# Block 1's first feed-forward products by Strassen's algorithm: pairs of output tiles in seven products of quarters

## The chip, the core and the metric
The kernel runs on one core of a Trainium2 chip. Its time is the device time of one launch in microseconds (us), the median of several runs. In the texts PE is TensorE, which multiplies matrices; ACT is ScalarE, DVE is VectorE, POOL is GpSimd, and SP is SyncE, which issues the loads of the weights. Every engine works through a list of instructions of its own, and the engines wait for each other by counting semaphores.

## What is computed
Two transformer blocks follow each other on one sequence of 512 tokens with 1024 features. The change touches the feed-forward layer of the first block, where `w_ff1` is 1024 by 4096 and `w_ff2` is 4096 by 1024:

```python
x = x + merged @ w_out[l]
h = rms_norm(x, g_mlp[l])
x = x + jnp.square(jax.nn.relu(h @ w_ff1[l])) @ w_ff2[l]
```

## The kernel before
**Halves.** Everything is float32. For a product of two matrices each operand is split in a high part that TensorE's fp32r format holds, and the rest. A product then takes three matmuls: high times high, weights' high times input's low, weights' low times input's high. The split of a weight tile costs one cast on ACT (raw `WR` to `WH`, L1226) and one subtraction on DVE (`WL = WR - WH`, L1691). There are four raw buffers `WR0` to `WR3` and three places for halves. A tile of weights is 128 by 1024 numbers.

**Order.** `tile_list` gives the order of all weight tiles: the output projection `wo` 0 to 7, then four quarters, each of 8 tiles `f1` and 8 tiles `f2`, then block 2. SP loads a tile as soon as the tile four before it has been split. ACT and DVE run two tiles ahead of PE with `split_to(tid[...] + 2)`, called at fixed places of their lists.

**Block 1's feed-forward.** A tile `f1, n` gives 128 hidden features for all 512 tokens: 8 chunks of 128 input features, three matmuls of 512 columns each, in PSUM bank 2 + n % 4. The input's halves are `Ah` and `Al`, made from x with its gain by `raw_high` (ACT, L1233) and `raw_low` (DVE, L1700) as the tiles of `wo` are added to x (DVE, L2037). The norm's factor is applied later, in the ReLU (DVE, L2172). It comes late: PE sums the squares in the middle of `f1` 0 and 1 (`sums("m1")`, the matmuls on ONE), DVE takes the variance (L1707), ACT a logarithm and an exponential (`root`, L1256 and L1258), DVE three operations of a Newton step (L1720 to L1724). ACT squares twice (L1528, and L1532 into `Bh`), DVE subtracts (`Bl`, L2177). The tiles `f2` multiply `Bh` and `Bl`, and DVE adds them to x (L2191).

**POOL** adds the squares of `wo`'s tiles for the norm (`add_squares`, L2381) and has nothing to do from there to the end of the third quarter.

## Time and profile before

| | |
|---|---|
| median of 3 runs | 1615.81 us (1610.54, 1617.73, 1615.81) |
| the profiled execution's own time | 1613.71 us |
| its span, first to last instruction | 1611.9 us |
| mean granted TensorE clock | 0.977 of 2.4 GHz |
| PE busy | 1542.1 us, 96% |
| DVE busy | 823.0 us, 51% |
| ACT busy | 617.6 us, 38% |
| POOL busy | 393.2 us, 24% |
| DMA | 154.11 MB, mean 96 GB/s |

Busy time is the share of the span in which an engine had an instruction in work. Matmuls overlap, so the time between the starts of two of them says more than the length of one. The chain of waits follows the end of the program back from each instruction to what released it.

### The profile page before, as it was taken

The page shows a single profiled execution, that of the slowest core. Times are in us where ns is not written, and L with a number is a line of the kernel's source. Part 1 is how long each engine was busy: PE and PEld are TensorE (multiplying, and loading weights), DVE is VectorE, ACT ScalarE, POOL GpSimd, SP SyncE. Part 2 cuts the span into 40 slices and gives each one's busy share as a digit, 9 for nine tenths or more (in the row PEclk, how much of TensorE's full clock was granted, in tenths as well). Part 3 has the DMA queues.
Part 4 walks back from the last instruction along what each step waited for, and adds up shares of the span by engine and source line. Part 5 has one row for each costly group of instructions (what it writes and reads, how often), then busy time and mean ns, then how long its engine had stood idle before and what let it go on. Part 6 is the DMA issues. An engine that isn't in the chain of part 4 may idle for free.

```text
span 1611.9 us, 19519 instructions
## 1 busy us (share of the span) xinstructions
PE 1542.1 (96%) x7198; PEld 1225.1 (76%) x7202; DVE 823.0 (51%) x1644; ACT 617.6 (38%) x1118; POOL 393.2 (24%) x364
## 2 busy tenths in 40 slices
PE   6899989999999999999999999989999999999995
PEld 5687665688877888888888788756687888888884
DVE  5537566444444334343446697577363543443444
ACT  5424456522334223232355433555443321322222
POOL 3200554300020000000036634566541210220112
PEclk9899999999999999999999999989999999999998
DMA  5743300323322333332322653311422333232321
GB/s 190 129 112 92 105 1 14 104 92 103 93 83 87 96 95 97 93 103 92 102 89 79 154 148 118 111 40 60 157 80 90 92 97 99 92 104 92 100 82 54
DMA packets 46669, 154.11 MB, mean 96 GB/s; under 512 B 5698, under 2 KB 5890, under 8 KB 46576
## 3 DMA queue, kind: packets, MB, share of 16 engines
q1 hardware_dynamic: 41840, 137.63, 27.2%
q0 software_dynamic: 4736, 15.25, 4.4%
q8 instruction: 58, 0.95, 0.3%
q14 instruction: 35, 0.29, 0.1%
HBM read 142.78 MB, written 9.55 MB: 95 GB/s over the span
## 4 chain that ended last, share of the span: by engine, by line
PE 86%; DVE 7%; ACT 3%; issue 2%; DMA 1%; DVEq 0%; SPq 0%; another core or an unknown queue 0%; POOL 0%; ACTq 0%
PE PSA L578 84%; PE PSA L780 2%; DVE WL L1691 1%; ACT AR L1298 1%; DVE AHL L1897 1%; DMA WR<-w_in 1%; PE PSA L924 0%; ACT AHL L1346 0%; DVE AR L1781 0%; DVE AR L1779 0%; DVE AR L1806 0%; DMA AR<-AR 0%; DVE AR L2367 0%; ACT WH L1226 0%; DVE AR L2274 0%
## 5 line engine op out<-in xcount | busy, mean ns | idle before, releaser
L578 PE MATMUL PSA<-Ah,WH 128*128 128x512 f32 x1072 | 426.0, 397 | 18.5 <-DVE WL L1691 18.5
L578 PE MATMUL PSA<-Al,WH 128*128 128x512 f32 x1072 | 421.2, 393 | 0.0
L578 PE MATMUL PSA<-Ah,WL 128*128 128x512 f32 x1072 | 420.8, 393 | 0.0
L1226 ACT CAST WH<-WR 128x1024 fp32r<-128x1024 f32 (+3 forms) x234 | 240.7, 1030 | 230.8 <-PE PSA L578 227.0
L1691 DVE TENSOR_TENSOR WL<-WR,WH 128x1024 fp32r<-128x1024 f32 (+3 forms) x207 | 252.6, 1221 | 72.7 <-ACT WH L1226 72.3
L578 PEld LDWEIGHTS PSA<-Ah,WH 128*128 128x128 f32 x1072 | 203.6, 190 | 64.8 <-issue 22.5
L578 PEld LDWEIGHTS PSA<-Ah,WL 128*128 128x128 f32 x1072 | 203.6, 190 | 43.3
L578 PE MATMUL PSA<-Bh,WH 128*128 128x512 f32 (+1 forms) x592 | 231.0, 390 | 5.7 <-DVE Bl L1968 4.0
L578 PEld LDWEIGHTS PSA<-Al,WH 128*128 128x128 f32 x1072 | 203.6, 190 | 42.6 <-issue 0.7
L578 PE MATMUL PSA<-Bh,WL 128*128 128x512 f32 (+1 forms) x592 | 229.8, 388 | 0.0
L578 PE MATMUL PSA<-Bl,WH 128*128 128x512 f32 (+1 forms) x584 | 227.1, 389 | 0.0
L2381 POOL TENSOR_TENSOR AR<-AR 128x512 f32<-128x512 f32 x36 | 51.8, 1445 | 572.6 <-ACT AR L1244 572.2
L578 PEld LDWEIGHTS PSA<-Bh,WH 128*128 128x128 f32 x592 | 111.9, 189 | 32.9 <-issue 10.8
L578 PEld LDWEIGHTS PSA<-Bh,WL 128*128 128x128 f32 x592 | 111.8, 189 | 22.8
L578 PEld LDWEIGHTS PSA<-Bl,WH 128*128 128x128 f32 x584 | 110.2, 189 | 22.0
L2544 POOL TENSOR_TENSOR AR<-AR 128x512 f32<-128x512 f32 x22 | 47.4, 2153 | 284.1 <-DVE AR L2343 284.1
L578 PE MATMUL PSA<-ARR,WH 128*128 128x512 f32 (+4 forms) x288 | 84.9, 380 | 1.4 <-DVE WL L1691 1.3
L2387 POOL TENSOR_TENSOR WL<-WR,WH 128x1024 fp32r<-128x1024 f32 (+1 forms) x27 | 64.3, 2385 | 84.8 <-ACT WH L1226 84.8
L2191 DVE TENSOR_TENSOR XT<-PSA,XT 128x512 f32<-128x512 f32 x32 | 22.1, 692 | 107.8 <-PE PSA L578 107.8
L2172 DVE SCALAR_TENSOR_TENSOR AR<-PSA,AR 128x512 f32<-128x512 f32 x32 | 22.1, 691 | 83.1 <-PE PSA L578 83.0
L1298 ACT ACTIVATE AR<-AR 128x512 f32<-128x512 f32 (+3 forms) x96 | 54.1, 564 | 24.1 <-DVE AR L1806 23.6
L578 PE MATMUL PSA<-AR 128*64 128x512 f32 (+10 forms) x220 | 61.5, 461 | 1.5 <-DVE AR L2261 1.0
(363 smaller groups left out, 1976.1 us busy)
## 6 DMA issues: line engine op xcount, KB each, us to landing
WR<-w_in SPq DMA_DIRECT2D x228, 512.0 KB, 3.5
gt_tmp<-AR SPq DMA_DIRECT2D x16, 256.0 KB, 2.1
WR<-w_in SPq DMA_DIRECT2D x8, 384.0 KB, 3.0
XT<-scr_tmp POOLq DMA_DIRECT2D x8, 264.0 KB, 11.4
XT<-xT_in SPq DMA_DIRECT2D x4, 512.0 KB, 8.1
XT<-scr_tmp POOLq DMA_DIRECT2D x8, 256.0 KB, 13.9
XT<-xT_in POOLq DMA_DIRECT2D x1, 2048.0 KB, 9.4
x_tmp<-XT POOLq DMA_DIRECT2D x1, 2048.0 KB, 7.6
```

What stands on the lines that cost most here:

```text
L578: return pe.matmul(o, l, r, start=start, stop=stop)
L780: last = pe.transpose(bank(3 + i % 2)[:, 128 * m:128 * m + 128], E1[i % 8][:, 128 * m:128 * m + 128], ident)
L1226: ac.copy(WH[p][:, 0:n], WR[j % RAW][:, 0:n]).then_inc(w_hi, 1)
L1298: ac.activation(E, E, ACT.Exp, bias=NMX1[:, c:c + 1], scale=-1.0, accum_out=RSM1[:, c:c + 1]).then_inc(p_ex, 1)
L1691: dv.tensor_tensor(WL[p][:, 0:n], WR[j % RAW][:, 0:n], WH[p][:, 0:n].bitcast(F), ALU.subtract).then_inc(w_lo, 1)
L1897: dv.tensor_tensor_reduce(E2[x][c][:, 0:n], scores2_at(i), bias, -1.0, NSK[:, h:h + 1] if x == "A" else 3e38, ALU.add, ALU.min, NMX2[:, c: ...
L2172: dv.scalar_tensor_tensor(out=RT[s], in0=bank(2 + n % 4), scalar=0.0, in1=RB["m1"], op0=ALU.max, op1=ALU.mult).then_inc(f_re, 1)
L2191: dv.tensor_tensor(x3[:, i, 0:T], bank(i % 2), x3[:, i, 0:T], ALU.add).then_inc(f_ad, 1)
L2381: pl.tensor_tensor(acc, acc, sq[(k - 1) % 3], ALU.add).then_inc(n_ac.sem, 1)
L2387: pl.tensor_tensor(WL[p][:, 0:n], WR[j % RAW][:, 0:n], WH[p][:, 0:n].bitcast(F), ALU.subtract).then_inc(w_lop, 1)
L2544: pl.tensor_tensor(ZR[s], RT[2 * s], RB["m2"], ALU.mult).then_inc(u_zr, 1)
```

## The change
The 32 tiles `f1` stay in the same order, but `f1` 2 to 31 are taken in 15 pairs. Weights of a pair (256 hidden features), input (1024 features) and output (512 tokens) are each cut in quarters, and seven products of 128 hidden features, 512 input features and 256 tokens (4 chunks of three matmuls of 256 columns) take the place of the eight of the plain way. This is Winograd's form of Strassen's algorithm.

- Four products need sums of quarters of the input (`TS`, their halves `TSH` and `TSL`). They are made once, during the tiles of `wo`: ACT writes x with its gain once more in float32 (`GX`), DVE does three operations on 256 columns for each two chunks and one that starts them, ACT casts and DVE subtracts 128 by 1024 four times.
- Three products need sums of quarters of the weights, made by POOL for each pair (`sums_of_weights`, four operations on 128 by 512). POOL also makes the low halves of the sixth and seventh left factor (`part_low`), DVE those of the first five.
- Places of halves are now half as large: six in `WH` and `WL` and four more in space of `wo`'s input.
- DVE joins the products (five additions from PSUM), then does the ReLU on a result in SBUF. ACT copies the first product out of PSUM. The first pair uses banks 2 and 3, which `f1` 0 and 1 used, and so waits for both their ReLUs (`f_re` 2); before, `f1` 2 and 3 used banks 4 and 5.

```diff
@@ build(): order of the products, their places @@
+    pairs = {tid["f1", n]: p for p, n in enumerate(range(2, 32, 2))}
+    firsts = {}
+    last_use = [0] * (2 * SPL + 4)
+    place, free_at, units, stop_of = {}, {}, [], {}
+    n_split = 0
     for j, (name, i, n, split) in enumerate(tiles):
-        n_mm_ += results.get(name, 1)
-        mm_no[j] = n_mm_
-        if split:
-            n_hi_ += 1
-            hi_no[j] = n_hi_
-            by_hi[n_hi_] = j
-            if name in pool_lo:
-                n_lop_ += 1
-                lo_no[j] = n_lop_
-            else:
-                n_lo_ += 1
-                lo_no[j] = n_lo_
+        n_split += split
+        if j in pairs:
+            firsts[j] = (n_hi_, n_lo_, n_lop_, n_mm_)
+            for m in range(7):
+                n_mm_ += 1
+                s = min(range(2 * SPL + 4), key=lambda s: last_use[s])
+                place[j, m], free_at[j, m], last_use[s] = s, last_use[s], n_mm_
+                units.append((j, m))
+            n_hi_, n_lo_, n_lop_ = n_hi_ + 7, n_lo_ + 5, n_lop_ + 2
...
@@ build(): the seven left factors of a pair @@
+        def part_of(j, m):
+            a, b, S = WR[j % RAW], WR[(j + 1) % RAW], WS[pairs[j] % 2]
+            return ((None, a[:, 0:512]), (1, b[:, 0:512]), (2, S[1]), (None, a[:, 512:1024]), (0, S[0]), (None, b[:, 512:1024]),
+                    (3, S[2]))[m]
...
@@ tensor_program @@
+            def product(j, m, b, c0, src):
+                c = firsts[j]
+                pe.wait_ge(w_hi, c[0] + m + 1)
+                if m < 5:
+                    pe.wait_ge(w_lo, c[1] + m + 1)
+                else:
+                    pe.wait_ge(w_lop, c[2] + m - 4)
+                ws = WPH[place[j, m]], WPL[place[j, m]]
+                for k in range(4):
+                    last = chunk(ws, src, k, bank(b)[:, c0:c0 + 256], 4)
+                last.then_inc(w_mm, 1)
+            def sums_of(t):
+                return (lambda k: TSH[k][:, 256 * t:256 * t + 256]), (lambda k: TSL[k][:, 256 * t:256 * t + 256])
+            def quarter(k0, c0):
+                return (lambda k: Ah[:, k0 + k, c0:c0 + 256]), (lambda k: Al[:, k0 + k, c0:c0 + 256])
+            def pair1(j):
+                p = pairs[j]
+                if p == 0:
+                    pe.wait_ge(f_re, 2)
+                    pe.wait_ge(f_dv.sem, f_dv.at("l3"))
+                else:
+                    pe.wait_ge(f_dv.sem, f_dv.at("c", 5 * (p - 1) + 1))
+                product(j, 0, 2, 0, quarter(0, 0))
+                product(j, 1, 2, 256, sums_of(2))
+                product(j, 2, 3, 256, sums_of(1))
+                product(j, 3, 3, 0, quarter(4, 0))
+                if p:
+                    pe.wait_ge(f_dv.sem, f_dv.at("c", 5 * (p - 1) + 3))
+                product(j, 4, 4, 256, sums_of(0))
+                product(j, 5, 4, 0, sums_of(3))
+                if p:
+                    pe.wait_ge(f_dv.sem, f_dv.at("c", 5 * (p - 1) + 4))
+                product(j, 6, 5, 0, quarter(4, 256))
...
@@ scalar_program @@
+                    if ph == 1:
+                        ac.activation(GX[i], x3[:, i, 0:T], ACT.Copy, scale=gain[:, i:i + 1]).then_inc(f_ac.sem, 1)
                     square(nm, i)
+                    if ph == 1 and i > 4:
+                        sums_high(i - 5)
+                if ph == 1:
+                    sums_high(3)
...
-            split_to(tid["f1", 2])
+            split_to(tid["f1", 1])
             root("m1")
-            split_to(tid["f1", 3])
+            split_units(stop_of[tid["f1", 1]] + 4)
+            ac.wait_ge(f_dv.sem, f_dv.at("x3", 2))
+            for n in range(2):
+                ac.wait_ge(f_re, n + 1)
+                squares1(n)
+                split_units(stop_of[tid["f1", 1]] + 5 + n)
...
+                    product_done(j, 1)
+                    if p > 1:
+                        ac.wait_ge(f_dv.sem, f_dv.at("c", 5 * (p - 2)))
+                    ac.copy(CU[n // 2 % 2][0], bank(2)[:, 0:256]).then_inc(f_ac.sem, 1)
+                    split_units(pair_stop(j, 1))
+                    product_done(j, 3)
+                    split_units(pair_stop(j, 3))
                     ac.wait_ge(f_re, n + 1)
-                    if n > 3:
-                        ac.wait_ge(f_lo, n - 3)
-                    ac.activation(RT[s + 1], RT[s], ACT.Square).then_inc(f_sq, 1)
-                    if q and i == 0:
-                        result(tid["f2", 8 * q - 1])
-                    ac.activation(Bh[:, i, :], RT[s], ACT.Square).then_inc(f_hi, 1)
-                    if n == 7:
+                    if q and n % 8 == 0:
+                        result(tid["f2", n - 1])
+                    squares1(n + 1)
+                    split_units(pair_stop(j, 5))
+                    ac.wait_ge(f_re, n + 2)
+                    squares1(n)
+                    split_units(pair_stop(j, 6))
...
@@ vector_program @@
+            def sums_low(k):
+                dv.wait_ge(f_ac.sem, f_ac.at(f"h{min(k, 2)}", k // 3))
+                dv.tensor_tensor(TSL[k], TS[k], TSH[k].bitcast(F), ALU.subtract).then_inc(f_dv.sem, 1)
+            def sums_of_input(i):
+                k = i % 4
+                t1, t2, t3, t4 = (TS[k][:, 256 * t:256 * t + 256] for t in range(4))
+                if i < 4:
+                    gained(i)
+                    dv.tensor_tensor(t1, GX[k][:, 256:512], GX[k][:, 0:256], ALU.subtract).then_inc(f_dv.sem, 1)
+                    return
+                if k:
+                    sums_low(k - 1)
+                gained(i)
+                dv.wait_ge(f_dv.sem, f_dv.at("d", k))
+                dv.tensor_tensor(t2, GX[4 + k][:, 256:512], t1, ALU.subtract).then_inc(f_dv.sem, 1)
+                dv.tensor_tensor(t3, GX[4 + k][:, 256:512], GX[k][:, 256:512], ALU.subtract).then_inc(f_dv.sem, 1)
+                dv.wait_ge(f_dv.sem, f_dv.at(f"x{k}", 0))
+                dv.tensor_tensor(t4, GX[4 + k][:, 0:256], t2, ALU.subtract).then_inc(f_dv.sem, 1)
...
+            split_to(tid["f1", 1])
+            sums_low(3)
             variance("m1")
-            split_to(tid["f1", 3])
+            split_units(stop_of[tid["f1", 1]] + 2)
             newton("m1")
+            split_units(stop_of[tid["f1", 1]] + 3)
+            for n in range(2):
+                result(tid["f1", n])
+                dv.scalar_tensor_tensor(out=RF[n], in0=bank(2 + n), scalar=0.0, in1=RB["m1"], op0=ALU.max, op1=ALU.mult).then_inc(f_re, 1)
+            split_units(stop_of[tid["f1", 1]] + 5)
...
+                    due = pair_stop(j, 1)
+                    split_units(due - 1)
+                    product_done(3)
+                    dv.wait_ge(f_ac.sem, f_ac.at("c", 3 * p))
+                    dv.tensor_tensor(RU[n // 2 % 2], halves(bank(3)), twice(c1), ALU.add).then_inc(f_dv.sem, 1)
+                    split_units(due)
+                    added(0)
+                    dv.tensor_tensor(u3, bank(2)[:, 256:512], u2, ALU.add).then_inc(f_dv.sem, 1)
+                    split_units(pair_stop(j, 3))
+                    product_done(5)
+                    added(1)
+                    dv.tensor_tensor(halves(second), halves(bank(4)), twice(u3), ALU.add).then_inc(f_dv.sem, 1)
+                    dv.tensor_tensor(u4, bank(4)[:, 256:512], u2, ALU.add).then_inc(f_dv.sem, 1)
+                    added(2)
+                    dv.scalar_tensor_tensor(out=second, in0=second, scalar=0.0, in1=RB["m1"], op0=ALU.max, op1=ALU.mult).then_inc(f_re, 1)
+                    product_done(6)
+                    added(3)
+                    dv.tensor_tensor(first[:, 256:512], bank(5)[:, 0:256], u4, ALU.add).then_inc(f_dv.sem, 1)
+                    added(4)
+                    dv.scalar_tensor_tensor(out=first, in0=first, scalar=0.0, in1=RB["m1"], op0=ALU.max, op1=ALU.mult).then_inc(f_re, 1)
+                    squares_low(n + 1, f_ac.at("c", 3 * p + 1))
+                    split_units(pair_stop(j, 5))
+                    squares_low(n, f_ac.at("c", 3 * p + 2))
...
@@ pool_program @@
+            def sums_of_weights(j):
+                p, (s1, s2, s4) = pairs[j], WS[pairs[j] % 2]
+                a, b = WR[j % RAW], WR[(j + 1) % RAW]
+                for jj in (j, j + 1):
+                    pl.wait_ge(w_ld[jj % RAW], 16 * (jj // RAW + 1))
+                if p > 1:
+                    pl.wait_ge(w_lo, firsts[of_pair[p - 2]][1] + 5)
+                if p == 1:
+                    pl.wait_ge(w_mm, mm_no[tid["wo", 7]])
+                def summed(s):
+                    pl.wait_ge(n_ac.sem, n_ac.at("weights", 4 * p + s))
+                pl.tensor_tensor(s1, b[:, 0:512], b[:, 512:1024], ALU.add).then_inc(n_ac.sem, 1)
+                pl.tensor_tensor(b[:, 0:512], a[:, 0:512], b[:, 0:512], ALU.subtract).then_inc(n_ac.sem, 1)
+                summed(0)
+                pl.tensor_tensor(s2, s1, a[:, 0:512], ALU.subtract).then_inc(n_ac.sem, 1)
+                summed(2)
+                pl.tensor_tensor(s4, a[:, 512:1024], s2, ALU.subtract).then_inc(n_ac.sem, 1)
+            def part_low(j, m):
+                s = place[j, m]
+                pl.wait_ge(w_hi, firsts[j][0] + m + 1)
+                pl.tensor_tensor(WPL[s], part_of(j, m)[1], WPH[s].bitcast(F), ALU.subtract).then_inc(w_lop, 1)
+            of_pair = sorted(pairs)
+            sums_of_weights(of_pair[0])
+            sums_of_weights(of_pair[1])
+            for p, j in enumerate(of_pair):
+                part_low(j, 5)
+                part_low(j, 6)
+                if p % 4 == 2:
+                    for jj in of_pair[p + 1:p + 3]:
+                        sums_of_weights(jj)
+                elif p % 4 != 1 and p + 2 < len(of_pair):
+                    sums_of_weights(of_pair[p + 2])
```

**Where instructions move.** DVE, tiles 5 to 7 of `wo` (L2037 and L2200 add a tile to x, WL is the low half of a coming weight tile, Al that of the input), before:

```order
L2037 TENSOR_TENSOR XT<-PSA,XT 128x512 [waits w_mm]
L1691 TENSOR_TENSOR WL1<-WR3,WH1 128x1024 [waits w_hi]
L1700 SCALAR_TENSOR_TENSOR Al<-XT,CST,Ah 128x512 [waits n_hi]
L2037 TENSOR_TENSOR XT<-PSA,XT 128x512 [waits w_mm]
L1691 TENSOR_TENSOR WL2<-WR0,WH2 128x1024 [waits w_hi]
L1700 SCALAR_TENSOR_TENSOR Al<-XT,CST,Ah 128x512 [waits n_hi]
```

And after, from tile 6 on (BHF holds the sums, ARR the halves of them):

```order
L2200 TENSOR_TENSOR XT<-PSA,XT 128x512 [waits w_mm]
L1850 TENSOR_TENSOR WL1<-WR3,WH1 128x1024 [waits w_hi]
L1863 SCALAR_TENSOR_TENSOR Al<-XT,CST,Ah 128x512 [waits n_hi]
L2211 TENSOR_TENSOR ARR<-BHF,ARR 128x1024 [waits f_ac]
L2225 TENSOR_TENSOR BHF<-BHF 128x256 [waits f_dv,f_ac]
L2226 TENSOR_TENSOR BHF<-BHF 128x256
L2228 TENSOR_TENSOR BHF<-BHF 128x256 [waits f_dv]
L2200 TENSOR_TENSOR XT<-PSA,XT 128x512 [waits w_mm]
L1850 TENSOR_TENSOR WL2<-WR0,WH2 128x1024 [waits w_hi]
L1863 SCALAR_TENSOR_TENSOR Al<-XT,CST,Ah 128x512 [waits n_hi]
```

Four operations stand between tile 6 and tile 7; the second WL of this piece is that of `f1` 1.

DVE, the norm of `f1` 0 and 1, before:

```order
L1691 TENSOR_TENSOR WL0<-WR1,WH0 128x1024 [waits w_hi]
L1707 TENSOR_SCALAR AR<-PSA 128x512 [waits n_ps]
L1691 TENSOR_TENSOR WL1<-WR2,WH1 128x1024 [waits w_hi]
L1720 TENSOR_TENSOR AR<-AR 128x512 [waits n_r]
L1722 SCALAR_TENSOR_TENSOR AR<-AR 128x512 [waits n_nr]
L1724 SCALAR_TENSOR_TENSOR AR<-AR 128x512 [waits n_nr]
```

And after:

```order
L1870 TENSOR_SCALAR AR<-PSA 128x512 [waits n_ps]
L1846 TENSOR_TENSOR WL0<-WR1,WH0 128x512 [waits w_hi]
L1846 TENSOR_TENSOR WL0<-WR2,WH0 128x512 [waits w_hi]
L1883 TENSOR_TENSOR AR<-AR 128x512 [waits n_r]
L1885 SCALAR_TENSOR_TENSOR AR<-AR 128x512 [waits n_nr]
L1887 SCALAR_TENSOR_TENSOR AR<-AR 128x512 [waits n_nr]
L1846 TENSOR_TENSOR ARR<-CTX,ARR 128x512 [waits w_hi,n_nr]
L2358 SCALAR_TENSOR_TENSOR AR<-PSA,AR 128x512 [waits w_mm] x2
```

The first halves of pair 0 now stand between the variance and the two ReLUs (L2358), and no whole tile does.

POOL after the squares of the norm (L2612; before, the next instruction there is again one of `add_squares`, for block 2):

```order
L2612 TENSOR_TENSOR AR<-AR 128x512 [waits n_ac,n_sq] x5
L2711 TENSOR_TENSOR CTX<-WR2 128x512 [waits w_ld2,w_ld1]
L2712 TENSOR_TENSOR WR2<-WR1,WR2 128x512
L2714 TENSOR_TENSOR CTX<-CTX,WR1 128x512 [waits n_ac]
L2716 TENSOR_TENSOR AR<-WR1,CTX 128x512 [waits n_ac]
L2711 TENSOR_TENSOR AR<-WR0 128x512 [waits w_mm,w_ld0,w_ld3]
```

The sums of pair 0 follow the squares at once; they wait only for raw tiles that SP has loaded by then.

## Rows read from the trace of the kernel before

**Rows 1.** The page's chain that ended last, by line

```profile
PE PSA L578 84%; PE PSA L780 2%; DVE WL L1691 1%; ACT AR L1298 1%; DVE AHL L1897 1%; DMA WR<-w_in 1%; PE PSA L924 0%; ACT AHL L1346 0%; DVE AR L1781 0%; DVE AR L1779 0%; DVE AR L1806 0%; DMA AR<-AR 0%; DVE AR L2367 0%; ACT WH L1226 0%; DVE AR L2274 0%
```

**Rows 2.** Busy time by stretches; columns: length, PE, PEld, DVE, ACT, POOL, clock, DMA

```profile
577.00:621.00 44.00, 44.00 (x204) 36.74 (x203) 19.49 (x25) 15.52 (x22) 0.00 (x0) 1.00 0.30 93
```

**Rows 3.** Timeline of PE, 512 columns; columns: start, length, engine, line, operation

```profile
84.75 0.39 PE L578 MATMUL PSA<-WH,Al 128*128 128x512 f32 x1
...
95.86 0.39 PE L578 MATMUL PSA<-WL,Ah 128*128 128x512 f32 x1
```

**Rows 4.** Timeline of PE, 288 columns

```profile
96.08 0.29 PE L578 MATMUL PSA<-WH,Ah 128*128 128x288 f32 x1
...
102.95 0.29 PE L578 MATMUL PSA<-WH,Al 128*128 128x288 f32 x1
```

**Rows 5.** Timeline of PE, 196 columns

```profile
851.26 0.27 PE L578 MATMUL PSA<-WH,Ah 128*128 128x196 f32 x1
...
852.15 0.27 PE L578 MATMUL PSA<-WL,Ah 128*128 128x196 f32 x1
```

**Rows 6.** Timeline of DVE and POOL, both reading two tiles of SBUF

```profile
857.23 2.42 POOL L2387 TENSOR_TENSOR WL<-WR,WH 128x1024 fp32r<-128x1024 f32 x1 [4.11 <-ACT WH L1226]
857.30 2.91 DVE L1720 TENSOR_TENSOR AR<-AR 128x528 f32<-128x528 f32 x1
```

**Rows 7.** Timeline of DVE and POOL, DVE reading PSUM and SBUF

```profile
886.90 2.51 POOL L2488 TENSOR_TENSOR XT<-XT,AR 128x512 f32<-128x512 f32 x2
888.96 1.28 DVE L2261 TENSOR_TENSOR AR<-PSA,AR 128x512 f32<-128x512 f32 x2
```

**Rows 8.** DVE's unblocked 320-column operation, and two DVE and two POOL in a row

```profile
865.05 0.49 DVE L2228 TENSOR_TENSOR AR<-AR 128x320 f32<-128x320 f32 x1
...
874.80 3.02 POOL L2488 TENSOR_TENSOR XT<-XT,AR 128x512 f32<-128x512 f32 x2
875.23 2.94 DVE L2245 TENSOR_TENSOR AR<-AR,CS 128x320 f32<-128x320 f32 x2
```

**Rows 9.** Timeline of all engines around tiles 6 and 7 of wo

```profile
479.83 0.69 DVE L2037 TENSOR_TENSOR XT<-PSA,XT 128x512 f32<-128x512 f32 x1 [2.95 <-PE PSA L578]
...
481.19 0.62 ACT L1244 ACTIVATE AR<-XT 128x512 f32<-128x512 f32 x1
481.57 0.75 DVE L1700 SCALAR_TENSOR_TENSOR Al<-XT,CST,Ah 128x512 fp32r<-128x512 f32 x1
481.71 1.04 ACT L1226 CAST WH<-WR 128x1024 fp32r<-128x1024 f32 x1
...
481.88 1.60 POOL L2381 TENSOR_TENSOR AR<-AR 128x512 f32<-128x512 f32 x1 [3.85 <-ACT AR L1244]
...
485.27 0.69 DVE L2037 TENSOR_TENSOR XT<-PSA,XT 128x512 f32<-128x512 f32 x1 [2.95 <-PE PSA L578]
485.88 1.21 DVE L1691 TENSOR_TENSOR WL<-WR,WH 128x1024 fp32r<-128x1024 f32 x1
...
487.46 0.47 PE L578 MATMUL PSA<-Ah,WH 128*128 128x512 f32 x1 [2.22 <-DVE WL L1691]
```

**Rows 10.** Timeline of all engines at the norm and f1 2

```profile
498.93 0.63 ACT L1258 ACTIVATE AR<-AR 128x512 f32<-128x512 f32 x1
...
500.19 0.39 PE L578 MATMUL PSA<-Ah,WH 128*128 128x512 f32 x1
...
501.99 0.69 DVE L1720 TENSOR_TENSOR AR<-AR 128x512 f32<-128x512 f32 x1
...
504.15 0.69 DVE L2172 SCALAR_TENSOR_TENSOR AR<-PSA,AR 128x512 f32<-128x512 f32 x1
```

**Rows 11.** Timeline of PE after its longest wait once started

```profile
72.02 0.79 PE L578 MATMUL PSA<-WH,Ah 128*128 128x512 f32 x1 [4.90 <-DVE AR L2080]
```

**Rows 12.** The same stretch by windows, columns as in Rows 2

```profile
72.10:76.40 4.30, 4.30 (x10) 3.39 (x11) 1.12 (x1) 0.00 (x0) 0.00 (x0) 0.50 1.03 133
```

**Rows 13.** Issues of loads: size, median us to landing

```profile
WR<-w_in SPq DMA_DIRECT2D x228, 512.0 KB, 3.5
```

More of the change, by code:

```diff
@@ new lines, in vector_program, with product_done, added @@
+            for n in range(2):
+                squares_low(n, f_ac.at("s", n))
+            for q in range(4):
+                for n in range(max(2, 8 * q), 8 * q + 8, 2):
+                    j = tid["f1", n]
+                    p, (c1, u2, u3, u4), first, second = pairs[j], CU[n // 2 % 2], RF[n % 4], RF[n % 4 + 1]
+                    def product_done(m):
+                        dv.wait_ge(w_mm, firsts[j][3] + m + 1)
+                    def added(m):
+                        dv.wait_ge(f_dv.sem, f_dv.at("c", 5 * p + m))
+                    due = pair_stop(j, 1)
[21 more added lines that the diff above has]
+                    squares_low(n, f_ac.at("c", 3 * p + 2))
+                    if n == 6:
@@ L2384, in weights_low @@
             def weights_low(j):
-                n, p = tiles[j][2], (hi_no[j] - 1) % SPL
+                n, p = tiles[j][2], place[j, 0]
                 pl.wait_ge(w_hi, hi_no[j])
```

171 lines of the change are left out of this document (117 added, 54 removed).

## The prediction
> **What bounds the kernel now.** I read the chain that ended last, then the busy times of the stretch that changes, then the timeline at its seams. In the chain the reader sees TensorE's matmul line with 84% of the span [rows 1]. In a quarter's eight f1 tiles PE is busy without a gap at full clock, DVE 19.5 of 44 us, ACT 15.5, POOL nothing [rows 2]. So every us that PE has less to do there is a us won, as long as nobody new makes PE wait. The timeline shows the two seams at which PE already depends on others: before f1 0, where it waits 2.22 us for the low half of f1 1 [rows 9], and at the end of f1 1, where it goes on to f1 2 at 500.19 although the first ReLU starts only at 504.15 [rows 10].
>
> **The matmuls.** The starts of 50 matmuls of 512 columns lie 11.11 us apart, 0.2267 us each [rows 3]; 53 of 288 columns 6.87 us, 0.1321 each [rows 4]; 11 in a row of 196 columns, from 851.03 on, 0.112 each, of which the first and last of nine are shown [rows 5]. From 512 to 288 columns a column costs 0.42 ns, from 288 to 196 only 0.22: the last are held up by something else that takes 0.112 each. The 256 columns of the change do not occur in such a stream. On the line through the first two points they cost 0.1187; the bounds are 0.112 and 0.132. I take 0.1187, since it is above the floor. A pair then has 7 x 12 = 84 matmuls, 9.97 us, for 48 x 0.2267 = 10.88: 0.91 us less, **13.6 us less for 15 pairs**. At 0.112 it would be 22 us less, at 0.132 3.3 us more. The Trainium skill, TensorE: Matmul & The Clock Gate, section Back-to-back issue gap, gives N / 2.4 + 2.5 ns for a warm matmul, 109 ns for 256 columns and 216 for 512; by it the estimate would be 18 us less, but its 216 is below the 227 ns measured here.
>
> **What the other engines get.** Per pair ACT has 7 casts, a copy and 4 squares at about 0.55 to 0.6 us a step (0.62 for 512 columns, and starts of consecutive ones are a tenth closer [rows 9]): 6.5 of 9.97 us. DVE has five low halves, two ReLUs and two Bl, 9 operations of 512 columns that read two tiles of SBUF, and five additions that read PSUM, two of 512 and three of 256 columns, for which I take 0.33: 9 x 0.61 + 2 x 0.61 + 3 x 0.33 = 7.7 us (512 columns are 0.69 long and the next starts 0.61 later [rows 9]). POOL has 6 operations, 1.25 us each [rows 7]: 7.5 us. Each fits alone. Together they don't. DVE's 528-column operation takes 2.91 instead of about 0.7 us and ends when POOL's is over plus half a us [rows 6]: two SBUF inputs on DVE and any POOL operation exclude each other. An operation that reads PSUM doesn't suffer: two take 1.28 us beside a busy POOL [rows 7]. And when both have queues they take turns: two DVE operations of 320 columns, 0.49 each alone, take 2.94 us between two of POOL, which take 3.02 [rows 8]; so one of each costs 1.47 us, and with 512 columns on DVE about 1.67, with 256 about 1.40. Each POOL operation thus costs a busy DVE 1.67 - 0.61 = 1.06 us. The Trainium skill, Perfetto Trace Analysis, section Optimizing Scalar/DVE Operations, warns of just this: moving work from DVE to GpSimd may not help since they share a port; this trace agrees [rows 6, 8].
>
> **Seam 1, before f1 0.** DVE now also does sums in tiles 4 to 7 of wo. In tile 5 it waits for ACT: the new copy (0.6), the square and a cast of 1024 columns (1.04) put its sums_low at 3.5 us after the tile's start and behind POOL's last addition to about 3.9, and it ends near 5.95 instead of within the 5.44 us of a tile: 0.5 late. In tile 6 the sums_low again ends at 5.1. By then POOL has added its last square (481.88 + 1.60 before [rows 9], 0.6 later now) and starts its four sums for pair 0, whose tiles have long landed (3.5 us per load [rows 13]). DVE's three 256-column operations take turns with three of them: 3 x 1.40 = 4.2, to 9.3. The addition of tile 7 starts 3.9 + 0.5 = 4.4 us late, and f1 1's low half waits 0.5 more for POOL's fourth. PE needs it: **4.9 us**, in a wait that is then 7.1 us long. What is queued behind on DVE (Al of chunk 7, more sums) is needed by PE's chunk 7 only, later. The bound from below is 0.3 us, if POOL gets in only when DVE is idle.
>
> **Seam 2, before the first pair.** The new wait for both ReLUs of f1 0 and 1. Their norm has its exponential at 498.93 + 0.63 = 499.56 [rows 10], 0.63 before f1 1 ends. Then ACT casts the first two parts (to 500.7), DVE makes their low halves (to 501.45), the Newton step takes 504.15 - 501.99 = 2.16 [rows 10], a third low half 0.6, two ReLUs 1.3: 505.55 instead of 500.19, **5.4 us** of PE idle. Nothing hides it; before, f1 2 and 3 did. Behind PE's wait stands all of pair 0. If all three low halves were free it would still be 3.5 us.
>
> **The clock.** PE came back from its 4.90 us wait at half clock: 0.50 granted, 10 matmuls in 4.30 us instead of 2.27 [rows 11, 12]. After the 2.22 us wait it did not [rows 9]. Both new waits are over 5 us, so I add 2.0 us twice, **4 us** (bounds 0 and 5).
>
> **The quarters.** In the second quarter's first two pairs POOL has 10 to 11 operations: four sums, two low halves, four sums, a low half. DVE must have the second addition of the quarter's second pair done when PE ends that pair at 19.96 us after the quarter's start. It cannot start on the casts before 3.85 (ACT waits for the second product). Up to that addition it has 13 SBUF operations (7.9 us) and 7 from PSUM (3.2), plus 10.5 POOL operations of which two or three lie beside PSUM work or waits: 8 x 1.06 = 8.5. 3.85 + 7.9 + 3.2 + 8.5 = 23.4, so PE waits about 3 us. The other two pairs have two POOL operations in all, and DVE recovers. The later quarters are alike, the first has sums and low halves in three pairs: 3 us each, **12 us**. Bounds: 0, and 26 if DVE never recovers (second rival). At a quarter's end the last ReLU, square and Bl take about 3 us after the last product, which 18 matmuls of f2's first tile (4.1 us) cover; f2's own work keeps its slack.
>
> **Sum.** 1613.7 (the profiled execution's own time) - 13.6 + 4.9 + 5.4 + 4 + 12 = 1626.4. The median of the runs shown is 2 us higher, so I say 1627, 0.7% over 1615.8.
>
> **Rivals.**
> - *The turns don't hurt.* POOL's operations fall in DVE's gaps, as its share of the time alone would allow. For it: both engines have idle time in every pair, and the halves are made one pair ahead. Against: they took turns where both had queues [rows 8]. Then only seam 2 and one drop of the clock remain: 1613.7 - 13.6 + 5.4 + 2 = 1607.5.
> - *VectorE becomes the bound of every pair* (slower side). 58 of POOL's 90 operations lie in f1 stretches (8 come before, 24 in f2's), 58 x 1.06 = 61 us on top of 15 x 7.7 = 115: 176 us for DVE against 150 of PE. It decides from the point where DVE's list is always behind; then 26 instead of 12: 1640. Against: low halves are made ahead in f2's stretches, whose DVE share is small.
> - *The columns are cheaper.* If 256 columns run at the floor [rows 5], PE has 8.5 us less; DVE then takes part of it back: 1618 to 1622.
> - *The saving doesn't exist*, at 0.132 us each: 1643. The line of two points speaks against it.
>
> **How the numbers follow.** My sum 0.58, first rival 0.18, second 0.12, cheaper columns 0.08, no saving 0.04. A difference under 0.5% (8 us, 1607.7 to 1623.9) can't be told from none by this measurement. My own case has the range 1617 to 1636, so 0.1 of its chance is "same" and the rest slower; the first rival is half faster, half same; cheaper columns are mostly same. Faster 0.11, same 0.24, slower 0.65. The range 1606 to 1641 takes in the first rival and most of the second.
>
> **What would show it.** Starts of 256-column matmuls 0.119 apart. PE idle about 7 us before f1 0, put down to DVE's low half, and about 5 before the first product of pair 0, put down to the ReLU, each followed by granted clock 0.5. In the quarters POOL operations of 1.5 us and longer and DVE operations of 1.5 to 2 us beside them, and waits of PE of some us before the third pair of a quarter. I am wrong if DVE's operations stay at 0.69 us beside POOL's, if f1 0 starts as early as now, or if f1 stretches last 40 us.

## The result, and the profile after

The changed kernel takes 1651.28 us (median of 4 runs, 1647.74 to 1655.99), the kernel before 1615.61 beside it: ratio 1.0227, 95% interval 1.0191 to 1.0264. It is slower, as forecast, but by 36 us where I said 11, and outside my range of 1606 to 1641. Timed again beside other kernels it was 1650.46 against 1612.57, ratio 1.0240 (1.0213 to 1.0268).

The profiled execution took 1649.6 us with a span of 1647.6, 35.7 more than before. From its start to the first matmul of `iq` (855.75 before, 891.21 after) the kernel has lost 35.46 of them, so nearly all of it lies in the stretch that the change touches or right at its ends. In the chain that ended last, by line, TensorE's matmul line has 73% where it had 84% [rows 1], and several lines of VectorE have come in:

```profile
PE PSA L648 73%; DVE WL L1846 2%; PE PSA L850 1%; DVE WL L1850 1%; DVE Bl L2370 1%; DVE ARR L1846 1%; DVE AR L1944 1%; ACT AR L1433 1%; ACT WH L1334 1%; DVE AR L1942 1%; PE PSA L994 1%; DMA WR<-w_in 1%; DVE AR L2405 0%; DVE AR L2397 0%; ACT
```

What PE waited for between 478 and 905, in the changed kernel (total us, times, longest). L2393 is the sum u3, which empties bank 2; L1850 the low half of `f1` 1; L1334 the cast of `ik` 0 (the first tile behind the last `f2`); L2358 the ReLU of `f1` 1; L2370 the low half of the squares; L2721 a low half made by POOL:

```profile
PE PSA L648 <- DVE AR L2393: 15.4, 7, 4.3
PE PSA L648 <- DVE WL L1850: 6.9, 1, 6.9
PE PSA L648 <- ACT WH L1334: 6.6, 1, 6.6
PE PSA L648 <- DVE AR L2358: 5.1, 1, 5.1
PE PSA L648 <- DVE Bl L2370: 1.2, 4, 0.3
PE PSA L648 <- POOL WL L2721: 0.6, 1, 0.6
```

The places of the large ones, in PE's timeline:

```profile
490.80 0.77 PE L648 MATMUL PSA<-Ah,WH 128*128 128x512 f32 x1 [6.92 <-DVE WL L1850]
...
510.55 0.58 PE L648 MATMUL PSA<-Ah,WH 128*128 128x256 f32 x1 [5.08 <-DVE AR L2358]
510.93 0.42 PE L648 MATMUL PSA<-Al,WH 128*128 128x256 f32 x1
...
512.00 0.41 PE L648 MATMUL PSA<-Ah,WH 128*128 128x256 f32 x1
...
591.82 2.68 PE L648 MATMUL PSA<-ARR 128*128 128x256 f32 x21
594.34 0.28 PE L648 MATMUL PSA<-Ah,ARR 128*128 128x256 f32 x1
...
626.76 0.39 PE L648 MATMUL PSA<-Ah,ARR 128*128 128x256 f32 x1 [4.31 <-DVE AR L2393]
```

The first one answers to the 2.22 us at the end of [rows 9]. The 21 matmuls from 591.82 on start 2.52 us apart from the next, so one of 256 columns costs 0.120 us at full clock. Behind the wait of 5.08 the starts from 510.93 to 512.00 lie 0.214 apart (five steps): half the clock. The windows show that clock (columns: length, PE, clock, DMA) behind two seams, in the fourth pair of the second and of the third quarter, and ahead of and in `ik` (0.50 is 1.2 GHz of 2.4):

```profile
490.00:492.00 2.00, 1.20 (x3) 0.50 0.24 57
...
511.00:513.00 2.00, 2.00 (x11) 0.50 0.00 0
...
628.00:631.00 3.00, 3.00 (x16) 0.50 0.78 296
720.00:723.00 3.00, 3.00 (x16) 0.50 0.74 277
869.00:873.00 4.00, 0.00 (x0) 0.63 0.00 0
873.00:877.00 4.00, 3.98 (x20) 0.52 0.82 283
```

The second quarter's f1 stretch took 48.41 us, for 45.31 before. This is its window in the changed kernel (columns as in [rows 2]); DVE is busy 40 us of 48, POOL 26, where the stretch of [rows 2] has 19.5 and 0 of 44:

```profile
590.02:638.43 48.41, 44.07 (x354) 43.68 (x352) 40.12 (x51) 19.28 (x37) 26.47 (x17) 0.96 0.27 98
```

The timeline of DVE and POOL in the third quarter shows why DVE is so busy: they take turns, and from start to start on either engine it is 1.70 us.

```profile
708.47 3.47 DVE L1846 TENSOR_TENSOR ARR<-WR,ARR 128x512 fp32r<-128x512 f32 x2
709.66 1.73 POOL L2721 TENSOR_TENSOR WL<-WR,WH 128x512 fp32r<-128x512 f32 x1
711.35 1.74 POOL L2721 TENSOR_TENSOR ARR<-AR,ARR 128x512 fp32r<-128x512 f32 x1
...
711.86 1.77 DVE L2370 TENSOR_TENSOR Bl<-AR,Bh 128x512 fp32r<-128x512 f32 x1
713.05 1.74 POOL L2721 TENSOR_TENSOR WL<-WR,WH 128x512 fp32r<-128x512 f32 x1
```

**Where the 35.5 us went**, by the starts of the stretches in both profiles. The matmuls of 15 pairs gave 12.0 (84 x 0.120 = 10.08 for 10.88). Lost were: 4.7 in the wait before `f1` 0 (6.92 for 2.22), 1.9 in `f1` 0 and 1 (14.67 for 12.73, clock 0.87), 5.1 before the first pair, 16.0 in eight waits within the quarters, 10.0 more in these f1 stretches (35.39, 48.41, 47.67 and 47.73 us long, clocks 0.93 to 0.96) beside their waits and matmuls, 2.6 in the four f2 stretches, 6.6 in a wait before `ik`, and 1.9 in `ik` at half clock. `wo` ended 1.4 earlier, which varies from run to run (3.8 later in after_again). Sum: 35.4. Of the 10.0 the clock has 7.8: by the starts, 82 matmuls ran at half clock in the four stretches and took 17.6 us in place of 9.8 (2.1 of the 7.8 behind the wait ahead of the first pair, then 1.5, 1.5 and 2.8 in the fourth pairs). The other 2.2 are some 0.27 for each of the eight waits; idle time is counted from the end of the last matmul, 0.28 after its start, where in a stream the next starts 0.12 after it, and the first one behind a wait is 0.23 from the next.

**A place that I had not looked at.** The 6.6 us before `ik` have nothing to do with the port. ACT's timeline of the kernel before has the cast of `ik` 0 (980 columns) two tiles ahead, and the next (588) one:

```profile
831.27 1.00 ACT L1226 CAST WH<-WR 128x980 fp32r<-128x980 f32 x1
...
836.71 0.67 ACT L1226 CAST WH<-WR 128x588 fp32r<-128x588 f32 x1
```

In the changed kernel all casts of `ik` come only at 870, behind a table load:

```profile
869.05 1.28 ACT L1386 ACT_TABLE_LOAD   x1
870.35 0.20 ACT L1386 ACTIVATE NS<-ONE 128x1 f32<-128x1 f32 x1
870.46 2.52 ACT L1334 CAST WH<-WR 128x980 fp32r<-128x980 f32 x3
```

The new planner gives each `f2` tile the place that was used longest ago, but `ik` 0 the place of the old fixed rotation, number 2. `f2` 31 happens to sit there, so the cast may start only when `f2` 31 is done. (Worked out from the planner's code: both get place 2; with the rule of e1_place `ik` 0 gets place 0.)

### The profile page after: what moved, and what is told of

Same layout as the page of the kernel before. It is cut to its first block, busy times and chain, and to the rows that moved or that the text cites. A ratio compares the mean times of both kernels' runs of the same rounds, so it can differ in the third digit from the quotient of the medians.

```text
span 1647.6 us, 21118 instructions
## 1 busy us (share of the span) xinstructions
PE 1541.0 (94%) x7742; PEld 1247.7 (76%) x7742; DVE 927.7 (56%) x1784; ACT 655.5 (40%) x1220; POOL 528.0 (32%) x454
## 4 chain that ended last, share of the span: by engine, by line
PE 76%; DVE 15%; ACT 5%; issue 3%; DMA 1%; DVEq 0%; POOL 0%; SPq 0%; ACTq 0%
PE PSA L648 73%; DVE WL L1846 2%; PE PSA L850 1%; DVE WL L1850 1%; DVE Bl L2370 1%; DVE ARR L1846 1%; DVE AR L1944 1%; ACT AR L1433 1%; ACT WH L1334 1%; DVE AR L1942 1%; PE PSA L994 1%; DMA WR<-w_in 1%; DVE AR L2405 0%; DVE AR L2397 0%; ACT AHL L1481 0%
## 5 line engine op out<-in xcount | busy, mean ns | idle before, releaser
L648 PE MATMUL PSA<-Ah,WH 128*128 128x512 f32 (+1 forms) x928 | 361.4, 389 | 30.9 <-DVE WL L1850 23.6
L648 PE MATMUL PSA<-Al,WH 128*128 128x512 f32 (+1 forms) x928 | 355.7, 383 | 0.0
L648 PE MATMUL PSA<-Ah,WL 128*128 128x512 f32 (+1 forms) x928 | 355.4, 383 | 0.0
L1334 ACT CAST WH<-WR 128x1024 fp32r<-128x1024 f32 (+2 forms) x204 | 209.4, 1029 | 191.1 <-PE PSA L648 185.7
L1850 DVE TENSOR_TENSOR WL<-WR,WH 128x1024 fp32r<-128x1024 f32 (+3 forms) x177 | 218.0, 1233 | 69.2 <-ACT WH L1334 68.6
L648 PEld LDWEIGHTS PSA<-Al,WH 128*128 128x128 f32 x928 | 177.8, 192 | 33.4 <-issue 0.7
L648 PEld LDWEIGHTS PSA<-Ah,WL 128*128 128x128 f32 x928 | 177.5, 191 | 33.7
L648 PE MATMUL PSA<-ARR,WH 128*128 128x256 f32 (+4 forms) x584 | 140.1, 333 | 2.5 <-DVE WL L1850 1.8
L2612 POOL TENSOR_TENSOR AR<-AR 128x512 f32<-128x512 f32 x36 | 50.2, 1402 | 278.7 <-ACT AR L1379 278.3
L648 PEld LDWEIGHTS PSA<-ARR,WH 128*128 128x128 f32 x584 | 99.2, 192 | 15.4 <-issue 2.7
L648 PE MATMUL PSA<-ARR,WL 128*128 128x256 f32 (+4 forms) x308 | 98.0, 330 | 0.0
L648 PE MATMUL PSA<-ARR 128*128 128x256 f32 (+10 forms) x424 | 77.0, 332 | 0.5 <-DVE AR L2060 0.5
```

What stands on the lines that cost most here:

```text
L648: return pe.matmul(o, l, r, start=start, stop=stop)
L1334: ac.copy(WH[p][:, 0:n], WR[j % RAW][:, 0:n]).then_inc(w_hi, 1)
L1850: dv.tensor_tensor(WL[p][:, 0:n], WR[j % RAW][:, 0:n], WH[p][:, 0:n].bitcast(F), ALU.subtract).then_inc(w_lo, 1)
L2612: pl.tensor_tensor(acc, acc, sq[(k - 1) % 3], ALU.add).then_inc(n_ac.sem, 1)
```

## The experiments

The theory: new waits stand at three seams (before `f1` 0, before the first pair, before `ik`) and in the quarters; the last come from DVE and POOL taking turns; each of the longer ones brings half clock. The rivals: the matmuls themselves or ACT are late; DVE has simply too many operations; the half clock has another reason. e1_place to e5_filler are each the changed kernel with the edit shown; e6_all joins three of them, e7_dve_lows goes on from e6_all, and e8_order and e9_tail from e7_dve_lows. Each profile is read by two stretches: from the end of `wo` 7 to the first product of a pair (14.95 before up to `f1` 2, 26.67 after), and from there to `iq` (355.56 before, 380.66 after).

| kernel | us | ratio to before | 95% | wo 7 to pair | pair to iq |
|---|---|---|---|---|---|
| e1_place | 1644.03 | 1.0197 | 1.0175 to 1.0220 | 26.73 | 371.84 |
| e2_seam1 | 1649.64 | 1.0230 | 1.0204 to 1.0257 | 22.89 | 381.13 |
| e3_banks | 1637.61 | 1.0160 | 1.0137 to 1.0183 | 22.14 | 373.27 |
| e4_pool_small | 1622.16 | 1.0068 | 1.0043 to 1.0092 | 26.96 | 357.00 |
| after_again | 1650.46 | 1.0240 | 1.0213 to 1.0268 | 27.07 | 381.13 |
| e5_filler | 1646.18 | 1.0214 | 1.0188 to 1.0240 | 26.66 | 378.86 |
| e6_all | 1627.66 | 1.0099 | 1.0072 to 1.0126 | 18.39 | 366.30 |
| e7_dve_lows | 1616.98 | 1.0019 | 1.0002 to 1.0037 | 18.39 | 356.32 |
| e8_order | 1618.39 | 1.0027 | 1.0009 to 1.0044 | 22.62 | 351.53 |
| e9_tail | 1611.35 | 0.9996 | 0.9980 to 1.0013 | 18.41 | 350.97 |

**e1_place**

```diff
-                if name == "f2":
+                if j > tid["f1", 1]:
                     p = min(range(SPL), key=lambda p: max(last_use[2 * p:2 * p + 2]))
```

> The changed kernel with one edit: every tile behind block 1's first two feed-forward tiles takes the place that was used longest ago, not only the f2 tiles. Theory (ACT's cast of ik 0 waits for the end of f2 31, since the fixed rotation gives ik 0 the place that f2 31 still uses): the wait of 6.60 us ahead of ik goes, and with it the half-clock stretch behind it (the ik products took 1.9 us longer in the changed kernel than before), so about 8.5 us less than the changed kernel's 1651.3, 1642.8. Rival (the cast is late because ACT is busy with the nx high halves and log_table, not because of the place): the wait stays at 5 us or more and the time at 1650 to 1652.

The wait before `ik` is gone, and ACT's timeline has its old order back:

```profile
858.38 1.00 ACT L1334 CAST WH<-WR 128x980 fp32r<-128x980 f32 x1
...
863.82 0.67 ACT L1334 CAST WH<-WR 128x588 fp32r<-128x588 f32 x1
```

Pair to iq is 8.8 us shorter than after, 9.3 shorter than in after_again. By the ratios of e1_place and of the changed kernel's two measurements the gain is 5 or 7, with 7 or 6 us on each side, so the medians alone hardly show the sign; it is read from the profile, where the wait and the half clock behind it (8.5 us together) are gone. The theory holds.

**e2_seam1**

```diff
+                if p == 0:
+                    pl.wait_ge(w_lo, lo_no[tid["f1", 1]])
```

> The changed kernel with one edit: GpSimd starts its weight sums for the first pair only when the low halves of the tiles f1 0 and f1 1 are done. Theory (those sums, 1.7 us each beside VectorE's operations of 512 columns, slow VectorE's norm and low halves by taking turns on a shared port): TensorE's wait of 6.92 us ahead of f1 0 shrinks to 2.5 to 3.5, and since a wait so short leaves the clock up, 2 more come back: 5 to 6 us less, 1645 to 1646. The sums come later, so the first pair's parts may be late by 1 to 3 us, which would be seen as a longer wait than 5.08 ahead of the first pair. Rival (VectorE's chain is long by its own count of instructions, the port costs nothing): the wait stays at 6.5 to 7 us and the time is that of the changed kernel or later.

The wait before `f1` 0 fell from 6.92 to 3.27 and the stretch up to the first pair by 3.8 us; the clock dropped behind 3.27 too, so the other 2 us did not come. The wait before the first pair stayed at 5.09. The medians, 1.0230 for 1.0227 and 1.0240, can't show 3.8 us. These are the DVE operations of this seam in the changed kernel, three sums of 256 columns in turn with POOL, 1.48 each, ahead of the addition for `wo` 7:

```profile
483.95 1.48 DVE L2225 TENSOR_TENSOR BHF<-BHF 128x256 f32<-128x256 f32 x1
485.35 1.48 DVE L2226 TENSOR_TENSOR BHF<-BHF 128x256 f32<-128x256 f32 x1
486.75 1.48 DVE L2228 TENSOR_TENSOR BHF<-BHF 128x256 f32<-128x256 f32 x1
488.15 0.68 DVE L2200 TENSOR_TENSOR XT<-PSA,XT 128x512 f32<-128x512 f32 x1
```

And the third of them in e2_seam1, where all three take 0.41:

```profile
480.83 0.41 DVE L2228 TENSOR_TENSOR BHF<-BHF 128x256 f32<-128x256 f32 x1
```

**e3_banks**

```diff
+                b = 2 if p % 2 else 6
...
-                    pe.wait_ge(f_dv.sem, f_dv.at("c", 5 * (p - 1) + 1))
-                product(j, 0, 2, 0, quarter(0, 0))
...
+                    pe.wait_ge(f_dv.sem, f_dv.at("c", 5 * (p - 2) + 1))
+                product(j, 0, b, 0, quarter(0, 0))
```

(likewise the next three products and their readers; the first pair no longer waits for the ReLUs but for the end of the norm, the second waits for the ReLUs; the sums of squares of the next norm, which bank 7 held, go to bank 0 with two more waits.)

> The changed kernel with one edit: the first four products of a pair go to banks 2 and 3 for every second pair and to 6 and 7 for the others, so that a pair starts when the sums of the pair ahead of the last are read, not those of the last. Theory (TensorE waits in the quarters for VectorE's u3, which frees bank 2, since VectorE is one pair behind): the seven waits of 15.4 us in all fall to under 4, the half clock behind four of them goes (about 8 us), and the wait ahead of the first pair, 5.08 for the rectified f1 1 in bank 3, falls to under 2 with its 2 us of half clock: 20 to 26 us less, 1625 to 1631. Rival 1 (VectorE and GpSimd together have more work than a quarter of four pairs lasts on TensorE, so the wait only moves to bank 4, to the weights' low halves or to the first f2 tile of each quarter): less than 12 us come back, and waits of 3 us and more stand in those places. Rival 2 (the two drops of the clock are not made by the waits): the waits go and the half clock stays, 1636 to 1640.

PE's waits from 478 to 905 in this kernel; L2376 is the low half of the squares, L2727 POOL's low halves:

```profile
PE PSA L648 <- DVE Bl L2376: 8.4, 4, 2.8
PE PSA L648 <- DVE WL L1856: 6.9, 1, 6.9
PE PSA L648 <- ACT WH L1340: 6.6, 1, 6.6
PE PSA L648 <- POOL ARR L2727: 2.9, 2, 2.4
```

The seam before the first pair went from 5.08 to 0.60, as the theory has it. The waits for u3 are gone, but 8.4 us stand now ahead of the seventh chunk of each quarter's first `f2` tile. From the pair to iq it is 7.4 us better, not 15 to 20: rival 1, in kind, since the waits moved, and both stretches together are 11.9 shorter (under 12); but no moved wait is as long as 3 us. The time of 1637.61 lies in the range of rival 2, whose mechanism is not there: in the f1 stretches the half clock stands only once more, behind a wait of 2.40 for POOL. The bank only set where PE feels that DVE and POOL are late.

**e4_pool_small**

```diff
-                pl.tensor_tensor(WPL[s], part_of(j, m)[1], ...
+                w = 512 if pairs[j] < 2 else 8
+                pl.tensor_tensor(WPL[s][:, 0:w], part_of(j, m)[1][:, 0:w], ...
```

(and the four weight sums likewise.)

> The changed kernel with GpSimd's weight sums and low halves done on 8 of 512 columns from the third pair on (so the outputs are not the reference's); instructions, semaphores and order are the same. Theory (VectorE is late in the quarters because its operations of 512 columns take turns with GpSimd's at 1.70 us a turn, 1.74 to 1.78 beside 0.69 alone): VectorE's low halves are 0.7 us again, the waits for u3 after the first quarter go (about 12 of the 15.4 us) with their half clock (6 to 8 us): 1631 to 1635, and the f1 quarters 2 to 4 end at 40.5 us each, or 2 to 3 less than before. Rival (VectorE's own count of operations per pair sets its pace, and the seven waits come from the shared banks alone): the waits stay above 8 us in all, the time above 1643.

Two rows of this kernel's timeline answer to the turns above; the second quarter's f1 stretch has its 51 DVE operations busy for 28.9 us, for 40.1 in the changed kernel; and PE's waits from 478 to 905 have u3 only once:

```profile
697.80 0.69 DVE L1846 TENSOR_TENSOR WL<-WR,WH 128x512 fp32r<-128x512 f32 x1
...
699.47 0.66 POOL L2732 TENSOR_TENSOR WL<-WR,WH 128x8 fp32r<-128x8 f32 x1 [9.27 <-ACT WH L1349]
```

```profile
586.44:628.53 42.09, 42.09 (x354) 42.08 (x352) 28.89 (x51) 19.48 (x37) 4.83 (x14) 1.00 0.28 97
```

```profile
PE PSA L648 <- DVE AR L2393: 0.2, 1, 0.2
```

With every DVE instruction still there, the quarters' waits are gone; 1622, 9 us lower than the theory asked. The last two quarters take 40.3 us for 43.52 before, 3.2 less, which is 4 x 0.80: the matmuls' saving is real, in full, once nobody is late. Pair to iq is 23.7 us shorter than in the changed kernel. That is the price of POOL's operations at full size, waits and clock together. This kernel takes away the turns and shortens POOL's own list at once; that the turns slow DVE is seen in its 51 operations, but how the 23.7 divide between a late DVE and a late POOL it does not show.

**after_again**

> The changed kernel itself once more, as the base for the kernels timed beside it: 1646 to 1652, the same seven waits for u3 (15.4 us), 6.9 ahead of f1 0, 5.1 ahead of the first pair and 6.6 ahead of ik.

1650.46, as expected; seven waits for u3 of 15.5 us, and 6.93, 5.08 and 6.60 at the seams.

**e5_filler**

```diff
+            def filler(n):
+                for i in range(n):
+                    mm(bank(7)[:, 0:256], Ah[:, 7, 0:128], Ah[:, 7, 0:256], True, True)
...
+                    filler(30)
                     pe.wait_ge(f_re, 2)
```

(and 40 on `Bh` ahead of `ik`.)

> The changed kernel with 30 matmuls of 256 columns, whose result nothing reads, ahead of the first pair, and 40 ahead of ik; they fill some 3.6 of the 5.08 us and 4.8 of the 6.60 us in which TensorE waits there. Theory (the half clock behind a seam comes from the idle time ahead of it): the waits that are left are 1.5 to 2, the pair and ik start when they did, and run at the full clock: the stretch from the first pair to the first f2 tile 35.4 to about 33.4, ik 18.2 to 16.3, in all 4 us less than the changed kernel. Rival (the clock falls for another reason, such as the new matmul shapes or the load of other engines): both stretches last as long as before, and the time is that of the changed kernel.

Two windows (columns as above), the first pair and `ik`; both at half clock in the changed kernel:

```profile
509.00:511.00 2.00, 1.92 (x16) 1.00 0.00 0
...
872.00:874.00 2.00, 2.00 (x21) 1.00 0.61 199
```

With 1.49 and 1.56 us idle in place of 5.08 and 6.60, PE keeps its clock: it is the idle time that costs it. `ik` took 16.4 us for 18.2. The stretch of the first quarter did not shorten to 33.4 but took 36.3: PE came faster to bank 2, waited 3.70 there for u3 where it had waited 2.59 in two waits, and lost its clock behind that wait. So the half clock in front of a late engine cost nothing here, and its return brought nothing. Both stretches together are 1.8 to 2.7 us shorter than in the two profiles of the changed kernel; the median is 4.3 under after_again's, as expected, but intervals of 4 us on each side can't tell these apart.

**e6_all**: the edits of e1, e2 and e3 together.

> The three edits of e1_place, e2_seam1 and e3_banks together in the changed kernel. In the profiles e1_place took 8.8 us out of the stretch from the first pair to iq, e2_seam1 3.8 between wo 7 and the first pair, and e3_banks 4.5 there and 7.4 behind it. Theory (they are separate places): the sum, 24 us less than the changed kernel, 1622 to 1627, still above the kernel before by 0.7 to 1.0%. Rival (one backlog of VectorE and GpSimd stands behind all of them, and what is taken out at one place comes back at the next): 1632 to 1638, with more than 12 us of waits for the squares' low halves ahead of the f2 tiles.

1627.66, just above the theory's 1622 to 1627, and 22.8 under after_again. Both stretches together are 22.6 us shorter than in the changed kernel (384.69 for 407.33), where I had added 24.5 from the single ones. So the three places hardly share anything.

**e7_dve_lows**: e6_all, and

```diff
-                    if j in pairs and m < 5:
+                    if j in pairs:
...
-                part_low(j, 5)
-                part_low(j, 6)
```

(the two calls are POOL's; the waits of PE, SP and POOL for these low halves go to DVE's counter.)

> As e6_all, and VectorE also forms the low halves of a pair's sixth and seventh weight, which GpSimd formed. Theory (the shared port sets the pace: a VectorE operation of 512 columns costs 0.69 alone and 1.74 with a GpSimd one in turn, so that VectorE loses 1.05 for every GpSimd operation; taking over two costs 1.4 and returns 2.1 a pair where both queues are full): the quarters' waits fall by a further 2 to 6 us, 1617 to 1623, though VectorE has 30 more operations to do. Rival (VectorE's number of operations sets the pace): 1.4 us more a pair in the quarters, the waits grow by 8 to 15, 1632 to 1638.

1616.98, at the lower end of the theory's range, 10.7 under e6_all, ratio to before 1.0019. Pair to iq fell by 10.0, for PE's waits for POOL (2.8 and 4.6 in e6_all) went, and the half clock with them: the four f1 stretches have a granted clock of 1.00. PE's four waits for DVE's squares stayed, 7.2 us for 7.3. So thirty operations more on DVE made the kernel faster, which refutes the rival; but what they took away is POOL's lateness, and that DVE had gained time by it, as the theory has it, this run does not show.

**e8_order**: e7_dve_lows, and

```diff
                     squares1(n + 1)
-                    split_units(pair_stop(j, 5))
+                    if n % 8 != 6:
+                        split_units(pair_stop(j, 5))
...
-                    if ph == 1:
+                    if ph == 1 and i == 7:
+                        sums_of_input(6)
+                    if ph == 1 and i != 6:
                         sums_of_input(i)
```

(the first hunk is ScalarE's; in VectorE's list the same split moves behind the low half of the second square.)

> As e7_dve_lows, with two changes of order. At a quarter's last pair ScalarE and VectorE square the pair's second tile before they split the next f2 weight, not behind it; and the input sums of the seventh wo tile come behind VectorE's work for the eighth. In e7_dve_lows VectorE's last low half of the squares starts at 711.01 behind a cast of 1.03 and a low half of 1.23, and TensorE waits 2.30 for it; and the addition for wo 7 starts at 482.34, behind three sums of 0.41. Theory: the waits ahead of the f2 tiles' seventh chunk (7.2 us in four) fall by about 1.3 each, to 2 in all; the wait ahead of f1 0 falls from 3.26 to about 2.2, which is what it was in the kernel before, and the half clock behind it (2 us) goes: 6 to 9 us less than e7_dve_lows, 1608 to 1611, or 0.1 to 0.3% under the kernel before. Rival (the order only moves the lateness to the f2 weight that is split later, or to the first pair's sums): the time of e7_dve_lows, 1615 to 1618.

Each edit did what it should where it stands: the waits ahead of the f2 chunks fell from 7.2 to 2.8, pair to iq by 4.8 us, and the wait before `f1` 0 is 2.22 with no drop of the clock. But the sums came back at the next seam, as a wait of 7.5 us ahead of the first pair for a low half (L1849), with half clock from 508.2 to 518.4. 1618.39 is the rival's time, and no better than e7_dve_lows:

```profile
PE PSA L647 <- DVE WL L1849: 7.5, 1, 7.5
PE PSA L647 <- DVE Bl L2375: 2.8, 4, 1.3
PE PSA L647 <- DVE WL L1853: 2.2, 1, 2.2
```

**e9_tail**: e7_dve_lows with the first hunk of e8_order, and

```diff
                     if n == 0:
+                        wait_norm("m1")(0)
+                        for i in range(12):
+                            mm(bank(7)[:, 0:256], Ah[:, 0, 0:128], Ah[:, 0, 0:256], True, True)
```

> As e7_dve_lows, with the order of e8_order at a quarter's last pair, but without its change to the input sums, whose lateness came back as a wait of 7.51 us ahead of the first pair; and with 12 matmuls of 256 columns, whose result nothing reads, in the wait ahead of f1 0. Theory: the stretch from the first pair to iq takes e8_order's 351.5 in place of e7_dve_lows' 356.3 (less 1 or 2 more, since no half clock stands behind a long wait ahead of the first pair), and the fillers leave 1.8 us of the 3.26 idle, so that f1 0 and f1 1 run at the full clock, 12.7 for them in place of 14.5: 6 to 7 us less than e7_dve_lows, 1609 to 1612, or 0.1% under the kernel before, hardly to be told from it. Rival (what is gained ahead of the first pair returns as a wait for its sums and low halves): 2 us more of that wait, and 1611 to 1614.

1611.35 against 1611.46: the kernel before, within 0.2%, and 39 us under the changed one. From the pair to iq it is 4.6 us faster than before (350.97), and from `wo` 7 to the pair 3.5 slower. The time lies in the ranges of both; the profile is against the rival, for the wait ahead of the first pair stayed at 0.60. The fillers missed: the clock fell all the same behind 1.87 us of idle time, and `f1` 0 and 1 took 14.5, not 12.7.

```profile
484.00:485.00 1.00, 0.00 (x0) 1.00 0.00 0
...
487.00:488.00 1.00, 1.00 (x4) 0.50 0.89 360
```

**When the clock falls.** The fillers of e5_filler, of the same kind, had kept the clock, and a wait of 1.9 us needs no fillers to be followed by half clock. The changed kernel's wait for u3 in the third pair of the first quarter kept the clock in its first profile and lost it in after_again. The row and the window behind it, first profile:

```profile
535.76 0.39 PE L648 MATMUL PSA<-Ah,ARR 128*128 128x256 f32 x1 [1.93 <-DVE AR L2393]
535.80:538.80 3.00, 3.00 (x25) 1.00 0.81 284
```

And in after_again:

```profile
541.50 0.58 PE L648 MATMUL PSA<-Ah,ARR 128*128 128x256 f32 x1 [1.92 <-DVE AR L2393]
541.60:544.60 3.00, 3.00 (x14) 0.50 0.83 285
```

And the trace of the kernel before has a drop behind a wait that is shorter than the 4.90 us of [rows 11]:

```profile
112.23 0.67 PE L1039 MATMUL PSA<-CST,AR 128*104 128x128 f32 x2 [3.30 <-DVE AR L2100]
112.00:116.00 4.00, 3.77 (x11) 0.50 0.00 0
```

It has more of them, behind waits of 2.03 (at 216.96), 1.83 (1069.52), 1.86 (1083.73) and 2.22 us (1229.62). In e3_banks the clock fell behind 2.40 (at 525.83) and 2.19 us (809.84) but not behind 2.69 (633.98) and 2.77 (722.27).

## Why the prediction was wrong

The sign was right, and so were the mechanisms of the terms that it had; the size was not: 1626.4 against the profiled 1649.6, 23.2 short. Two drops of the clock where six came, quarter waits that were too short, and a wait with no term at all make 20.4 of it. By its own terms:

- **The matmuls**, -13.6: measured -12.0, since 256 columns cost 0.120 and not 0.1187. e4_pool_small shows the term alone. 1.6 of the 23.2.
- **Seam 1**, +4.9 in a wait of 7.1: measured +4.7 in one of 6.92. Cause shown by e2_seam1, which took 3.65 of the 4.70 away, and by the three sums of 1.48; e8_order, which moved the sums, took the rest.
- **Seam 2**, +5.4: measured +5.1. Cause shown by e3_banks: without the wait for the ReLUs 0.60 is left, for a low half.
- **The clock**, +4: this step failed. It counts two drops, at the seams, and those two cost what it said, 1.9 in `f1` 0 and 1 and 2.1 behind the wait ahead of the first pair. Four more came: 1.5, 1.5 and 2.8 behind the quarter waits of 4.31, 3.70 and 3.50 us, and 1.9 in `ik`. Measured 11.6, so 7.6 of the 23.2. The prediction gave its own four quarter waits of 3 us no drop and said no reason; its only rows on the clock were the waits of 4.90 and 2.22 us, and the drop behind 3.30 us stood in the trace of the kernel before.
- **The quarters**, +12: this term was mis-sized. Measured 16.0 in waits and 2.2 around them, 6.2 of the 23.2. Three of the eight are 3.5 to 4.3 us, each ahead of the fourth pair of its quarter, where I had expected the third's; the small ones had no place in my count. The turns hit the ReLUs too, which read two tiles of SBUF: 1.01 us in the mean of 14 (L2405), and 0.69 in e4_pool_small.
- **What had no term**: the place of `ik` 0, 6.6, shown by e1_place. The planner gives the f2 tiles their places by a new rule, and the tile behind them takes its place by the old one; the prediction says nothing of either. Then 2.6 in the f2 stretches, of which 1.2 are four waits of 0.3 for Bl, and against it 1.4 that `wo` ended earlier. 0.5 lie behind iq.

The rival that put DVE's bound at 1640, with 26 us in the quarters, had the better picture: what POOL's operations cost there, waits and clock together, is 23.7 (e4_pool_small), and DVE and POOL are behind in every quarter (e3_banks: with other banks the lateness stays until the f2 tile). It lacked the clock as a term and the place of `ik` 0. The rival that the saving doesn't exist is refuted by e4_pool_small. That DVE's number of operations alone is the limit is refuted by e7_dve_lows.

The Trainium skill, Perfetto Trace Analysis, section Optimizing Scalar/DVE Operations, warns that moving operations between DVE and GpSimd might not help since they share a port. The runs agree: e7_dve_lows moves work back, from GpSimd to DVE, and wins 10.7 us.
